# Gated prompt stage: solved 16x16 blocks sent from memory straight to the diagonal, buffers cleared by ScalarE instead of a spread by GpSimd

## The reference, cut to what matters

```python
G = jnp.cumsum(gc, axis=-1)
gamma = jnp.where(tril, jnp.exp(jnp.where(tril, diff, 0.0)), 0.0)
M = jnp.where(strict, jnp.einsum('nbhid,nbhjd->nbhij', kb, kc) * gamma, 0.0)
Tinv = lax.linalg.triangular_solve(eye + M, jnp.broadcast_to(eye, M.shape), left_side=True, lower=True)
u = Tinv @ (vc * bc[..., None])
wk = Tinv @ (kb * jnp.exp(G)[..., None])

def step(S, inp):
    qi, ki, ui, wi, Gi, Ai = inp
    v_new = ui - wi @ S
    o = (qi * jnp.exp(Gi)[..., None]) @ S + Ai @ v_new
    Gl = Gi[..., -1:]
    S = S * jnp.exp(Gl)[..., None] + jnp.einsum('bhcd,bhce->bhde', ki * jnp.exp(Gl - Gi)[..., None], v_new)
    return S, o
```

## Time and profile before

| | us |
|---|---|
| median of three runs | 4831.57 |
| the profiled execution | 4820.32 |
| its span | 4818.6 |
| TensorE busy | 4018.3 (83% of the span) |
| VectorE busy | 2273.1 (47%) |
| GpSimd busy | 1376.9 (29%) |
| ScalarE busy | 918.1 (19%) |

### The profile page before, as it was taken

How to read it: one execution, slowest core, us unless ns; L and a number is a source line. 1 busy time by engine, 2 the same in 40 slices (tenths; PEclk the granted TensorE clock), 3 DMA queues, 4 the chain that set the end, 5 groups by cost and what they waited for, 6 DMA issues and landing times. The chain is left out here.

```text
span 4818.6 us, 65654 instructions
## 1 busy us (share of the span) xinstructions
PE 4018.3 (83%) x24608; PEld 3736.8 (78%) x24608; DVE 2273.1 (47%) x4007; ACT 918.1 (19%) x1703; POOL 1376.9 (29%) x1020
## 2 busy tenths in 40 slices
PE   8995677864696778799999979985887579999996
PEld 8995566843575457799999969984786379999996
DVE  3113667523332222655555556514772346556554
ACT  2000222111332110211111122202452011111112
POOL 3222444321200002332332223223452224233331
PEclk9997677855777889899999989986886689999998
DMA  4222110002103321211111022223322111111111
GB/s 157 84 84 94 38 38 23 7 19 79 41 0 108 117 95 35 61 35 48 48 35 48 17 56 90 72 76 74 76 50 58 57 34 54 43 52 44 35 44 45
DMA packets 354076, 273.42 MB, mean 57 GB/s; under 512 B 103998, under 2 KB 316158, under 8 KB 353551
## 3 DMA queue, kind: packets, MB, share of 16 engines
q1 hardware_dynamic: 314726, 227.64, 16.1%
q10 hardware_dynamic: 39212, 43.95, 2.7%
HBM read 215.48 MB, written 58.34 MB: 57 GB/s over the span
## 5 line engine op out<-in xcount | busy, mean ns | idle before, releaser
L928 PE MATMUL fup_acc<-ffn_high,fup_wh 128*128 128x364 f32 (+1 forms) x2112 | 698.3, 331 | 11.3 <-DVE ffn_low L1033 3.4
L929 PE MATMUL fup_acc<-ffn_low,fup_wh 128*128 128x364 f32 (+1 forms) x2112 | 697.2, 330 | 0.0
L930 PE MATMUL fup_acc<-ffn_high,fup_wl 128*128 128x364 f32 (+1 forms) x2112 | 694.8, 329 | 0.0
L928 PEld LDWEIGHTS fup_acc<-ffn_high,fup_wh 128*128 128x128 f32 x2112 | 399.5, 189 | 13.2 <-issue 8.9
L930 PEld LDWEIGHTS fup_acc<-ffn_high,fup_wl 128*128 128x128 f32 x2112 | 399.5, 189 | 0.0
L929 PEld LDWEIGHTS fup_acc<-ffn_low,fup_wh 128*128 128x128 f32 x2112 | 399.5, 189 | 0.0
L1090 DVE TENSOR_TENSOR trunk_xT<-fup_dn,trunk_xT 128x364 f32<-128x364 f32 x528 | 282.7, 535 | 246.3 <-PE fup_dn L946 246.3
L944 PE MATMUL fup_dn<-fup_gh,fup_dh 128*128 128x364 f32 (+1 forms) x1056 | 348.7, 330 | 21.3 <-issue 21.3
L945 PE MATMUL fup_dn<-fup_gl,fup_dh 128*128 128x364 f32 (+1 forms) x1056 | 347.6, 329 | 0.0
L946 PE MATMUL fup_dn<-fup_gh,fup_dl 128*128 128x364 f32 (+1 forms) x1056 | 347.0, 329 | 0.0
L322 PE MATMUL p_acc<-p_wh,even_in_high 128*128 128x296 f32 (+1 forms) x936 | 281.5, 301 | 10.6 <-DVE even_in_low L360 7.9
(11 more groups left out here) (731 smaller groups left out, 9103.4 us busy)
## 6 DMA issues: line engine op xcount, KB each, us to landing
fup_ws<-in_ffn_w_up SPq DMA_DIRECT2D x88, 512.0 KB, 3.8
fup_ds<-in_ffn_w_down SPq DMA_DIRECT2D x22, 1024.0 KB, 5.9
fs_kp<-in_cache_fox_k SPq DMA_DIRECT2D x64, 256.0 KB, 2.8
fs_vp<-in_cache_fox_v SPq DMA_DIRECT2D x64, 256.0 KB
ev<-p_o ACTq DMA_DIRECT2D x104, 148.0 KB, 1.8
p_ws<-in_ev_w_in SPq DMA_DIRECT2D x12, 1184.0 KB, 6.4
qkv<-gqkv_conv ACTq DMA_DIRECT2D x24, 544.0 KB
gqkv_ws<-in_od_w_in SPq DMA_DIRECT2D x24, 512.0 KB, 4.2
```

The lines of the kernel that those rows point to most:

```text
L928: pe.matmul(ps, wh[:, b, k], xh[:, k, c0:c0 + w_], start=(k == 0), stop=False)
L929: pe.matmul(ps, wh[:, b, k], xl[:, k, c0:c0 + w_], start=False, stop=False)
L930: mm = pe.matmul(ps, wl[:, b, k], xh[:, k, c0:c0 + w_], start=False, stop=(k == KD - 1))
```

## The change

The compact buffers `Xc` and `XcT` and the function `expand` on GpSimd are gone. The sixteen DMAs of `scatter_blocks` write each solved block straight to its place on the diagonal in `XX`, which the new helper `diagonal(n, r)` addresses: partitions r, side n, all 8 heads, columns r of each head. The zeros off the diagonal are made by ScalarE: a new function `clear(i, side)` copies a zero, broadcast from a tile of two columns, over a whole side of `XX` (128 partitions x 1024). The clear of the transposed side of chunk t + 1 stands behind `copy_w(t-1)`, ahead of `copy_product(t, 2)`; the clear of side 0 stands last in the turn, behind `square_y(t-1)`. `clear` takes over the waits that `expand` had for the old contents. SyncE waits for the clear of a side before it issues the eight DMAs of that side, and TensorE's first product and first join wait for the DMAs instead of `expand`.

```diff
-        Xc, XcT = (ph.sb(n, [P, H, BASE]) for n in ("Xc", "XcT"))
+        zero = ph.sb("zero", [P, 2])
...
+        def diagonal(n, r):
+
+            return XX[r, n].rearrange("p g (h t) -> p (g h) t", t=P)[:, :, r]
...
                 sp.wait_ge(s["x_out"], 32 * (i + 1))
-                if i:
-                    sp.wait_ge(s["xt_set"], 2 * i)
-                    sp.wait_ge(s["x_set"], 2 * i)
+                sp.wait_ge(s["xt_clear"], i + 1)
                 for b in range(NBLK):
                     r = slice(b * BASE, (b + 1) * BASE)
-                    sp.dma_start(XcT[r], xt_d[b].rearrange("h c r -> c h r")).then_inc(s["xct_in"], 16)
+                    sp.dma_start(diagonal(1 + i % 2, r), xt_d[b].rearrange("h c r -> c h r")).then_inc(s["xct_in"], 16)
+                sp.wait_ge(s["x_clear"], i + 1)
                 for b in range(NBLK):
                     r = slice(b * BASE, (b + 1) * BASE)
-                    sp.dma_start(Xc[r], x_d[b].rearrange("h r c -> r h c")).then_inc(s["xc_in"], 16)
+                    sp.dma_start(diagonal(0, r), x_d[b].rearrange("h r c -> r h c")).then_inc(s["xc_in"], 16)
...
-                        pe.wait_ge(s["xt_set"], 2 * i + g + 1)
+                        pe.wait_ge(s["xct_in"], 16 * NBLK * (i + 1))
...
-                        pe.wait_ge(s["x_set"], 2 * i + g + 1)
+                        pe.wait_ge(s["xc_in"], 16 * NBLK * (i + 1))
...
+            def clear(i, side):
+
+                if i == 0:
+                    act.wait_ge(s["zeroed"], 4)
+                empty = zero[:].unsqueeze(2).to_broadcast([P, 2, HF * P])
+                if side:
+                    if i >= 2:
+                        act.wait_ge(s["w_sum"], 2 * (i - 2) + 2)
+                    act.copy(XX[:, 1 + i % 2], empty).then_inc(s["xt_clear"], 1)
+                else:
+                    if i:
+                        act.wait_ge(s["x_sum"], 2 * TOP * i)
+                    act.copy(XX[:, 0], empty).then_inc(s["x_clear"], 1)
...
                 if old:
                     copy_w(t - 1)
+                if has(t + 1):
+                    clear(t + 1, 1)
                 if now:
                     copy_product(t, 2)
                 if old:
                     gate_z(t - 1)
                     square_y(t - 1)
+                if has(t + 1):
+                    clear(t + 1, 0)
...
+            pool.memset(zero[:], 0.0).then_inc(s["zeroed"], 1)
...
-                    expand(t + 1, 1)
                     low_quarter(t + 1)
-                    expand(t + 1, 0)
```

More of the change, by code:

```diff
@@ L3171, in gdn_prompt @@
                  "w_out o_sum o_out s_sum s_scaled s_added y_sq my_done ry_done z_done y_scaled y_done y_turned mixed out "
-                 "low_out blocks_out sub_in sub_done x_out xc_in xct_in x_set xt_set dve_step").split()
+                 "low_out blocks_out sub_in sub_done x_out xc_in xct_in xt_clear x_clear dve_step").split()
         s = {n: ph.sem(n) for n in names}
@@ L3593, in mask_q @@
                                        bc(C["tri"][:], 1, HF), ALU.mult).then_inc(s["q_masked"], 1)
[L3595 to L3610, removed]
             def scale_state(i):
```

## The result

The median of seven runs after is 4860.7 us (4845.8 to 4869.4), against 4831.6 us (4823.1 to 4835.2) for seven runs before on the same chip: a ratio of 1.0054, with a 95% interval from 1.0041 to 1.0067. The medians differ by 29 us; the interval of the ratio is 20 to 32 us. The profiled execution took 4848.6 us (span 4846.9) against 4820.3 before: 28.3 us more. The two lie 12 and 11 us under their medians.

A forecast was written before the change was run, and what follows sets the result against it. No engine is full; a chain of waits through SyncE's queue, between last masked product and gather, bounds the kernel. Chunk 2's 4.7, chunks 3 to 6's 28.8 and chunk 7's 2.9 sum to 36.4 us: forecast 4868 us, range 4852 to 4882.

The forecast's parts named there:

- signs named: Side-0 issues right after the clear, gather some 7 us after the masked product, VectorE idle 8 to 10 us, turn 49 us.
- Parts 1 and 2: 32 spreads leaving GpSimd: worth 0 on the path; 16 clears joining ScalarE: 1.06 us each, side 0 clear at 3445.7.
- Part 3: SyncE's queue: loads and gather stand behind the wait for side 0's clear; chunk 4's gather starts 6.8 us later.
- Part 4: Gather to subN issue, now right behind the loads: 7.2 us instead of 6.36, +0.8 us in chunk 4.
- Part 5: VectorE's first substitution steps, later, escape GpSimd's masking: 0.5 us back for chunk 4, 1.9 for chunk 7, none for 2.
- A larger cost: Rival: gather waits out the loads and stretched steps stay, +44 us, 4875; with clears of 2.49 us +52, 4884; chance 0.13.
- The clock turns: Rival: TensorE's four other turns run fast, 4.9 us each, +17, 4849 us; or the fast one slow, 4873; chance 0.20.
- Hidden: Rival: slack before the substitution takes up the delay, 4832 us; chance 0.02.
- Faster: Rival: side-0 transfers leave before the last masked product, gather starts as before, only gains remain, 4824 us; chance 0.03.

The follow-up runs named there:

- wait_only: The kernel before with only SyncE's wait for the last join and the squares of y added ahead of the side-0 transfers: 4863.5 us, 1.0071.
- clear_early: The changed kernel with ScalarE's clear of side 0 ahead of the squares of y instead of behind them: 4854.4 us, 1.0040.
- side0_spread: The changed kernel with side 0 as before (own buffer, GpSimd's spreads), only the transposed side cleared and written directly: 4848.0 us, 1.0029.
- loads_first: The changed kernel with SyncE's qk and v loads issued before the sixteen transfers: 4846.4 us, 1.0037.
- act_issue: The changed kernel with the eight side-0 transfers issued from ScalarE's queue, right behind its clear: 4827.8 us, 0.9995.
- act_issue_loads: The changed kernel with side 0's transfers issued by ScalarE and the qk and v loads ahead of side 1's transfers: 4814.5 us, 0.9966.
- before_loads: The kernel before with only SyncE's qk and v loads moved ahead of the transfers: 4830.6 us, 0.9997.
- best_early: act_issue_loads with ScalarE's clear of side 0 and its transfer issues ahead of the squares of y: 4857.7 us, 1.0052.
- warm: The changed kernel with the matmuls of the level-0 join of chunks 1 to 6 done three times over: 4874.6 us, 1.0092.

## Why the prediction was right, and where its terms were off

The mechanism, its place and the sign were as written, and *wait_only* shows that the wait in the queue alone is enough for the loss. 4860.7 us lies 7 us under the forecast of 4868 and inside its range. That it came so near is partly luck: the delay of the gathers was forecast 13 us too small and what comes back 23 us too small, and the two errors have opposite signs. Of the signs named, the start of the side-0 issues, the clears, the first steps and VectorE's idle time (8.9 to 9.4 us in chunks 3 to 6) came true; the gathers are 9 to 9.7 us late instead of 7, and a turn takes 46.2 us, not 49. The terms, in the profiled executions, where the change cost 28.3 us:

```
chunk                                        2      3      4      5      6      7
gather behind the end of the last
masked product, after, us                   7.7    9.6    9.7    9.0    9.6    5.4
gather start to subN issue, after, us       6.8    6.7    6.6    6.9    6.6    5.2
first substitution step, start, before  3376.67 3411.62 3454.12 3497.05 3538.97 3582.28
first substitution step, start, after   3381.58 3427.15 3477.23 3522.43 3572.52 3610.77
```

*Parts 1 and 2, clears.* Right: 1.05 and 1.03 us against 1.06. But the squares of y ended 0.2 us behind the masked product (3458.81 + 0.19 = 3459.00 against 3458.77), not 0.66 ahead of it, and side 0 was clear 1.2 us behind it instead of 0.6.

*Part 3, the queue.* The step is right and its size too small. Against 0.0 to 0.5 us before, the gathers of the six chunks are 48.5 us later in sum, where 3.8 + 4 x 6.8 + 4.8 = 35.8 had been forecast. In chunk 4 it is 9.7 us from masked product to gather, not 7.3. Of the 2.4 us, 0.6 are the later clear, 0.6 the transfers' issues, which took 4.36 instead of 3.8, and 1.2 the row load: I had taken its 0.34 us of the earlier trace rows, an issue into an idle queue, while right behind v's it takes 1.56.

*Part 4, what the gather meets.* From gather to subN 6.6 to 6.9 us in chunks 2 to 6, not 7.2; over six chunks 5.4 us more than before, against some 4. The base was uneven, which one turn could not show: before, chunks 5 and 6 had taken only 5.0 and 5.2 us, chunk 4 6.4. The rule of the Trainium skill on completion order (DMA: Bandwidth & Descriptors, section Queues, rings and completion order) would have made it 7.9. It did not, but the row load's own landing is in no row, so the rule itself is neither shown nor refuted here.

*Part 5, what comes back.* This is the term that failed: 3.9 us forecast. From the first step of a chunk to the next masked product, over the six turns and the tail up to the state's output, 27.2 us came back. 48.5 + 5.4 - 27.2 = 26.7 us, against 26.45 measured between chunk 1's first step and the state's output (chunk 1's began 0.84 later; some 1 us lies behind the stage).

Two parts of the 27.2 have rows. One is VectorE: 228.3 us busy before and 217.7 after (the windows at the top), 10.6 less, with the same work. How much of it lies on the path isn't shown. The groups by shape that lost most, before and then after (columns: total busy us, mean ns; then idle time):

```profile
L3651 DVE TENSOR_TENSOR gd_subP<-gd_subN,gd_subX 64x1 f32<-64x1 f32 x6 | 4.7, 776 | 9.9 <-issue 6.2 <-DMA gd_subN<-blocks_d 3.8
L3651 DVE TENSOR_TENSOR gd_subP<-gd_subN,gd_subX 64x225 f32<-64x225 f32 x7 | 7.6, 1091 | 0.2
L3708 DVE TENSOR_TENSOR gd_sneg<-gd_rm,odd_gp_nbeta 128x2 f32<-128x2 f32 x24 | 12.6, 524 | 0.8
```

```profile
L3654 DVE TENSOR_TENSOR gd_subP<-gd_subN,gd_subX 64x225 f32<-64x225 f32 x7 | 3.8, 538 | 0.2
L3711 DVE TENSOR_TENSOR gd_sneg<-gd_rm,odd_gp_nbeta 128x2 f32<-128x2 f32 x24 | 8.9, 369 | 0.8
```

I had looked for stretched steps beside the masking only, at the start of the substitution (there the first step is now 0.15 us in all six chunks, as forecast). The last step of a substitution (64x225) and the small operations of the masked products (128x2) were stretched too. Only part of that was beside the spreads: seven of the eleven long 128x2 operations before were, 0.9 to 1.05 us each instead of 0.16. The three long 64x225 steps, 1.1 to 2.2 us, ran beside GpSimd's scaling of the state or its `level`, which the change keeps, and had started behind them:

```profile
3463.75 2.15 DVE L3651 TENSOR_TENSOR gd_subP<-gd_subN,gd_subX 64x225 f32<-64x225 f32 x1
3463.60 1.90 POOL L3616 TENSOR_TENSOR gd_S<-gd_S,odd_gp_eg 128x1024 f32<-128x1024 f32 x1 [8.81 <-PE gd_PS L3366]
```

The other four, and all seven after, are alone or start ahead of GpSimd's instruction, and take 0.53 to 0.55 us.

That a VectorE instruction with two inputs in SBUF contends with a GpSimd instruction that reads it is what the Trainium skill says (SBUF — State Buffer, section Who interferes with whom), and these rows agree; the mistake was to price it at one place.

The other part is the clock, a rival of the prediction that could come "wholly or in part": two of the four turns with a slow stretch before now ran fast. The prediction's price, 4.9 us a turn, is too low for these two: they took 14.3 and 14.1 us before and 8.1 after, 12.1 us together. TensorE after, a slow turn and a fast one, answers to the earlier trace rows (first gram, third product):

```profile
3439.51 1.10 PE L3308 MATMUL gd_PS<-gd_qk 128*128 128x256 f32 x4 [3.02 <-DVE gd_vb L3690]
...
3452.54 1.14 PE L3330 MATMUL gd_PS<-gd_XX,gd_low 64*64 64x64 f32 x16
...
3490.07 1.10 PE L3308 MATMUL gd_PS<-gd_qk 128*128 128x256 f32 x4 [2.95 <-DVE gd_vb L3690]
...
3498.19 1.14 PE L3330 MATMUL gd_PS<-gd_XX,gd_low 64*64 64x64 f32 x16
```

13.0 us and 8.1, as in the earlier trace rows. But the gaps before them are nearly the same, 3.02 and 2.95 us, and the turn after, behind 2.95 us again, took 13.0. So the prediction's reason, a longer gap, does not decide here. Whether it does elsewhere can be counted. The stretch from first gram to third product is there in five turns with a solve in each of the eleven traces. In 20 of the 55 it takes 8.1 us, at a granted clock of 1.00 (2.4 GHz), in the others 13.0 to 14.6 us, at a mean of 0.54 to 0.61, which means mostly 1.2 GHz:

```
run                 slow turns of 5    the five stretches together, us
before                     4                  62.6
the change                 2                  50.4
wait_only                  3                  57.9
clear_early                3                  55.4
side0_spread               3                  56.6
loads_first                5                  67.6
act_issue                  1                  47.0
act_issue_loads            2                  51.5
before_loads               5                  70.1
best_early                 5                  70.3
warm                       2                  52.3
```

Behind a gap of at most 1.2 us all 17 turns were fast, behind one of 3.0 us or more all 30 were slow, and behind one of 2.95 to 2.98 us three were fast and five slow. So gap and clock go together as the prediction had it, but no run set the gap alone, and what decides at 2.95 us stays open. The table is of one execution each, so it can't be set against medians; it does show that 10 to 20 us between two traces can be slow turns and not the edit. It may also have to do with the spread of the kernel after, 24 us over seven executions against 12 for the kernel before, though larger sets of the latter spread over up to 19. With 10.6 and 12.1 taken from the 27.2 us, some 4 to 5 are not attributed, more where VectorE's gain is off the path. A buffer of its own for side 0 in each of two turns, which would free the transfers of their wait in SyncE's queue, was not tried.

*The rivals.* "A larger cost" did not come: the gather took 6.6 to 6.9 us and not 7.9, the first steps were not stretched, a clear took 1.05 us and not 2.49. What was dearer than forecast, the row load's issue and the late squares, is in none of its terms. "The clock turns" came in part, with two turns, beside the delay and not in its place. "Hidden" is excluded by VectorE's 9 us of idle time. "Faster" was rightly excluded for this change: it needed a gather on time, and with the side-0 transfers in another queue and the loads moved it got that.

## What to carry to other kernels

A wait on an engine's queue is paid by everything behind it, also by transfers that have nothing to do with it: list them, and look for the one that the critical path waits for. When an edit of this kind loses, try the same wait in the queue of the engine that does the awaited work before giving the edit up: here the change costs 29 us with the eight issues in SyncE's queue, nothing with them in ScalarE's, and gains 18 with two loads moved besides. The same eight issues one place earlier on ScalarE, ahead of work that VectorE waits for, cost 26. A change in what one engine does, or when, can stretch or free the instructions of its neighbour; compare the neighbour's mean times by shape over the whole stage, not at one place. And before a difference of 10 or 20 us between two traces is put down to the edit, count the slow turns of TensorE in both.

## What the runs showed of the hardware

Issuing a large load takes longer right behind another. SyncE issues the 512 KB row load in 0.34 us when it had been waiting, in 0.43 us right behind eight small transfers, and in 1.5 to 2.1 us right behind the issue of v's load; v's own, behind qk's 1 MB, takes 1.6 to 2.1 us in these turns.

The gathers of 8 KB are slowed by loads in front of them. In chunks 3 to 6, from the first gather's issue to subN's: 4.8 to 5.9 us right behind the row load alone (*loads_first*), 6.4 to 7.9 behind qk, v and row load, 2 MB (the change, *wait_only*, *clear_early*), and 7.8 to 8.9 behind the same 2 MB with eight small transfers of ScalarE's queue beside them (*act_issue*). With those beside them and the row load alone ahead it is 5.9 to 7.3 (*act_issue_loads*). Each figure is from one execution of a run.

A VectorE step of 64x225 with two inputs in SBUF took 0.53 to 0.55 us alone or when it started ahead of GpSimd's scaling of the state, and 1.1 to 2.2 us when it started behind that or behind the `level` (the kernel before, the change, *loads_first*, *act_issue_loads*, *before_loads*: 13 long ones, 10 short ones with an overlap).

ScalarE clears 128x1024 f32 from a broadcast zero in 1.03 to 1.05 us.

A granted clock of 0.50 can hold through 20 us of TensorE without a pause (*warm*), and a pause of 2.95 us before the grams can be followed by either level.
